# Two engines' work re-ordered around the feed-forward chunks and the norms, a weights-stationary last input stage, and an end by column halves

## The chip, the cores and the metric

The kernel runs on one core of a Trainium2 chip. The metric is the device time in microseconds (us) of one launch of the whole program; lower is better. TensorE (PE in the profile) multiplies, VectorE (DVE) and ScalarE (ACT) do the elementwise work, GpSimd (POOL) issues small loads and some elementwise work, SyncE (SP) issues the large DMAs.

## What is computed

Two transformer-like blocks on 256 tokens of width 1024, all in float32, batch 1:

```
x = x + 0.5*norm(swiglu(norm(x)))          # ffn1: 1024 -> 2*2816 -> 1024
x = x + norm(token_mixing(norm(x)))        # retention + neighbourhood attention
x = x + 0.5*norm(swiglu(norm(x)))          # ffn2
x = x + recurrent_mixer(norm(x))           # "a": 1024 -> 2*1536, conv, gated scan, -> 1024
x = x + shortconv_mixer(norm(x))           # "b"
return norm(x)

def shortconv_mixer(h):                    # WIDTH = 1536
    bg, cg, xv, gate = split(h @ w_in, 4)  # w_in is 1024 x 6144
    y = bg * causal_depthwise_conv(cg * xv, conv_w)     # 3 taps
    return (y * silu(gate)) @ w_out        # 1536 -> 1024
```

`norm` is an RMS norm over the 1024 columns with a gain.

## The kernel before

**Every product in two parts.** A float32 operand is split into a rounded high part and a low part, and a product is hi*hi + hi*lo + lo*hi, three matmuls into one accumulation. Activations sit transposed in `xT_hi` and `xT_lo` (in `xT`, side by side). All weights come as one stream of 151 groups of 1 MB (`raw`, a ring of 6 slots). ACT makes `w_hi` of a group (`round_group`, L450), then DVE makes `w_lo` in the place of `raw` (`low_group`, L872). `round_to(n)` on ACT and `low_to(n)` on DVE do all groups below n that are not done yet: where these calls stand in the two engines' programs is the order by hand that the change moves. Every engine runs its program in order and waits on semaphores (`wait_ge`). PE waits for `lo_done` before it uses a group.

**Two forms of an input stage.** In the column form (`column_tile`, matmuls L1416 to L1418) the activations of 128 tokens are stationary and 512 columns of weights stream; a column is two groups, 2 token tiles x 8 chunks x 3 = 48 matmuls of 512. The result has tokens on the partitions and has to be transposed. In the chunk form (`chunk`, L1613 and L1615) the weights are stationary: for 128 output columns, `w_hi` with `xT_hi` and `xT_lo` at once (512 wide) and `w_lo` with `xT_hi` (256 wide), 8 times; a chunk is one group, gate half and up half, 32 matmuls. Here the hi*hi+lo*hi part lies in columns 0 to 255 and the hi*lo part in 256 to 511 of the bank, and they must be added (ACT copies the second, L585 and L587; DVE adds the first, L1035 or L1038 and L1040), but nothing is transposed.

**Stages.** `f1_in` (2 columns, then 18 chunks), `f1_out`, `mix_in`, three small output stages, `f2_in`, `f2_out`, `a_in`, `a_out`, `b_in` (12 columns), `b_out`. For each chunk of `f1_in` and `f2_in`, ACT runs round_to, `chunk_round` of the chunk before (L597), `second_parts`, `chunk_silu` (L592), and DVE runs low_to, `chunk_low` of the chunk before (L1052), `chunk_sums`, `chunk_product` (L1046); in f1 the sums have one operation more (L1036, the token's scale).

**Joints.** Between stages stands `norm(n)`. PE ends the output stage with token tile t=1, transposes the normed tile t=0 within it, and starts on the next stage's first column with t=0, for which it needs `xT_hi` (ACT L460) and `xT_lo` (DVE L900, `take_lo`) of that tile. In `norm`, DVE runs `low_to(after + 3)` for t=0 ahead of the two `take_lo`. Half way through the second column's t=0 tile PE transposes the normed tile t=1 (`xn_ready`, from DVE L933).

**b_in before.** Twelve columns; ACT takes the gate (L832, L833), DVE multiplies into `b_prod` (L1357), PE transposes (`b_transposes`, L1849, 4 matmuls of 128), DVE runs the 3-tap convolution out of PSUM (L1370 to L1373), ACT and DVE make `yT_hi` and `yT_lo` (L838, L1378).

**End before.** `norm(*NORMS[5])`: for each token tile, DVE adds (L925), ACT sums squares and takes the root (L468, L470), DVE inverts (L930) and scales two halves (L933), SP stores each (L354).

## Time and profile before

| what | value |
|---|---|
| device time, median of 3 runs (lowest to highest) | 913.71 us (913.54 to 915.02) |
| the profiled execution's own time | 913.96 us |
| its span, first to last instruction | 912.2 us |
| PE busy | 897.5 us, 98% of the span, 4550 matmuls |
| PE weight loads busy | 759.2 us, 83% |
| DVE busy | 602.1 us, 66%, 742 instructions |
| ACT busy | 470.8 us, 52%, 630 instructions |
| POOL busy | 75.2 us, 8% |
| DMA | 168.87 MB, 185 GB/s on average |
| granted TensorE clock | 0.999 of full speed |

Busy time of an engine is the union of its instructions; matmuls overlap in the records, so the pace of PE is read from the starts of successive matmuls or from stretches with a known number of them. The column of a chain of waits gives for each piece what the end was waiting for.

### The profile page before, as it was taken

Reading aid. Unit: us, or ns where it says so; the run is one execution under the profiler, and the core shown is the slowest. Engines: PE = TensorE matmul, PEld = TensorE weight load, DVE = VectorE, ACT = ScalarE, POOL = GpSimd, SP = SyncE. Lnnn points to the kernel's source line nnn. Section 1 sums busy time; section 2 is a strip of 40 time slices with the busy share of each in tenths; the row PEclk is TensorE's granted clock in tenths of the full one; section 3 lists DMA queues with packets and bytes.
Section 4 is the critical chain, followed back from the end, with each engine's and each line's share of the span. In section 5 each row is a group of like instructions: output and inputs, shape, how many; then the busy total and the mean of one; then the engine's idle time right before and its main releaser. Section 6 shows DMA issues by size and latency. Waiting matters only on the chain.

```text
span 912.2 us, 11249 instructions
## 1 busy us (share of the span) xinstructions
PE 897.5 (98%) x4550; PEld 759.2 (83%) x4550; DVE 602.1 (66%) x742; ACT 470.8 (52%) x630; POOL 75.2 (8%) x103
## 2 busy tenths in 40 slices
PE   8999999999999999999999999999999999999996
PEld 6888887878888888888788888887999888888885
DVE  6677777466666646748657667446879866666653
ACT  6655556445533446435555556435787544444441
POOL 3000000003232210000000000000290000000000
PEclk9999999999999999999999999999999999999999
DMA  9755554547544534455565555546535356554421
GB/s 341 286 188 187 181 185 181 185 185 266 189 144 175 172 128 155 152 187 188 200 227 186 185 185 182 198 160 242 193 133 185 139 181 257 185 184 185 185 93 46
DMA packets 25843, 168.87 MB, mean 185 GB/s; under 512 B 3408, under 2 KB 3584, under 8 KB 6592
## 3 DMA queue, kind: packets, MB, share of 16 engines
q1 hardware_dynamic: 23040, 159.46, 47.9%
q0 software_dynamic: 2752, 8.69, 2.9%
q8 instruction: 36, 0.59, 0.3%
q14 instruction: 15, 0.12, 0.0%
HBM read 167.09 MB, written 1.05 MB: 184 GB/s over the span
## 4 chain that ended last, share of the span: by engine, by line
PE 81%; DVE 9%; ACT 6%; DMA 2%; issue 1%; SPq 0%; DVEq 0%
PE acc L1416 19%; PE acc L1418 19%; PE acc L1417 19%; PE acc L1613 7%; DVE w_lo L872 5%; ACT w_hi L450 4%; PE acc L1615 4%; PE aux L1800 1%; DMA raw<-weights 1%; PE acc L1437 1%; DVE gate_c L1036 1%; PE aux L1416 1%; PE aux L1418 1%; PE aux L1417 1%; ACT gate_c L592 1%
## 5 line engine op out<-in xcount | busy, mean ns | idle before, releaser
L872 DVE TENSOR_TENSOR w_lo<-raw,w_hi 128x2048 fp32r<-128x2048 f32 x148 | 338.5, 2302 | 161.9 <-ACT w_hi L450 161.7
L450 ACT ACTIVATE w_hi<-raw 128x2048 fp32r<-128x2048 f32 x146 | 276.4, 1911 | 51.6 <-DMA raw<-weights 51.4
L1416 PE MATMUL acc<-w_hi,xT 128*128 128x512 f32 x512 | 203.4, 397 | 2.7 <-DVE xT L900 1.7
L1613 PE MATMUL acc<-xT,w_hi 128*128 128x512 f32 x576 | 201.9, 396 | 0.0
L1418 PE MATMUL acc<-w_hi,xT 128*128 128x512 f32 x512 | 199.8, 390 | 0.0
L1417 PE MATMUL acc<-w_lo,xT 128*128 128x512 f32 x512 | 199.4, 390 | 0.0
L1615 PE MATMUL acc<-xT,w_lo 128*128 128x256 f32 x576 | 160.1, 278 | 0.0
L1613 PEld LDWEIGHTS acc<-xT,w_hi 128*128 128x128 f32 x576 | 108.0, 188 | 26.4 <-issue 1.0
L1416 PEld LDWEIGHTS acc<-w_hi,xT 128*128 128x128 f32 x512 | 96.2, 188 | 22.9 <-issue 4.1
L1418 PEld LDWEIGHTS acc<-w_hi,xT 128*128 128x128 f32 x512 | 96.1, 188 | 20.6
L1417 PEld LDWEIGHTS acc<-w_lo,xT 128*128 128x128 f32 x512 | 96.3, 188 | 18.8
L1615 PEld LDWEIGHTS acc<-xT,w_lo 128*128 128x128 f32 x576 | 108.3, 188 | 0.0
L1416 PE MATMUL acc<-w_hi,hT_hi 128*128 128x512 f32 x176 | 68.8, 391 | 1.3 <-DVE w_lo L872 1.3
L1418 PE MATMUL acc<-w_hi,hT_lo 128*128 128x512 f32 x176 | 68.5, 389 | 0.0
L1417 PE MATMUL acc<-w_lo,hT_hi 128*128 128x512 f32 x176 | 68.5, 389 | 0.0
L592 ACT ACTIVATE gate_c<-gate_c 128x256 f32<-128x256 f32 x36 | 14.9, 415 | 49.2 <-DVE gate_c L1036 46.4
L1416 PEld LDWEIGHTS acc<-w_hi,hT_hi 128*128 128x128 f32 x176 | 33.0, 188 | 8.6 <-issue 1.7
L1418 PEld LDWEIGHTS acc<-w_hi,hT_lo 128*128 128x128 f32 x176 | 33.0, 188 | 6.8
L1417 PEld LDWEIGHTS acc<-w_lo,hT_hi 128*128 128x128 f32 x176 | 33.0, 188 | 6.8
L1416 PE MATMUL acc<-w_hi,yT_hi 128*128 128x512 f32 x96 | 37.6, 392 | 0.3 <-DVE yT_lo L1293 0.3
L1815 PE MATMUL acc<-xT,w_hi 128*128 128x256 f32 x128 | 37.4, 292 | 0.0
L1418 PE MATMUL acc<-w_hi,yT_lo 128*128 128x512 f32 x96 | 37.4, 390 | 0.0
(222 smaller groups left out, 1066.4 us busy)
## 6 DMA issues: line engine op xcount, KB each, us to landing
raw<-weights SPq DMA_DIRECT2D x149, 1024.0 KB, 4.8
gain_pre<-gains POOLq DMA_DIRECT2D x5, 512.0 KB, 5.1
bias_raw<-bias_in POOLq DMA_DIRECT2D x32, 64.0 KB, 3.5
gain_post<-gains POOLq DMA_DIRECT2D x3, 512.0 KB, 4.4
gate_w<-gate_w_in POOLq DMA_DIRECT2D x1, 1536.0 KB, 8.8
x<-x_in SPq DMA_DIRECT2D x4, 256.0 KB, 5.8
raw<-weights SPq DMA_DIRECT2D x2, 512.0 KB, 5.6
out<-tmp SPq DMA_DIRECT2D x4, 256.0 KB, 2.1
```

The lines of the kernel that those rows point to most:

```text
L450: a.activation(w_hi[:, g % RING], raw[:, g % RING], ACT.Copy).then_inc(hi_done, 1)
L592: a.activation(gate_c[:, n % 2], gate_c[:, n % 2], ACT.Silu).then_inc(silu_ready, 1)
L872: v.tensor_tensor(w_lo[:, slot], raw[:, slot], w_hi[:, slot].bitcast(F32), ALU.subtract)\
L1036: v.tensor_tensor(gate_c[:, b], gate_c[:, b], rstd0_row[:], ALU.mult).then_inc(gate_summed, 1)
L1416: m.matmul(dst, hi[:, k, cols], w_hi[:, slot, w], start=first, stop=False)
L1417: m.matmul(dst, hi[:, k, cols], w_lo[:, slot, w], start=False, stop=False)
L1418: return m.matmul(dst, lo[:, k, cols], w_hi[:, slot, w], start=False, stop=last)
L1437: i = m.matmul(acc[:, t, 0], xT[:, k, t * P:(t + 1) * P], w[:, g, unit * UNIT:(unit + 1) * UNIT], start=k == 0 and xT is xT_hi and w is w_ ...
L1613: m.matmul(dst, w_hi[:, slot, w], xT[:, k].rearrange("p a q -> p (a q)"), start=k == 0, stop=False)
L1615: i = m.matmul(dst[:, 0:S], w_lo[:, slot, w], xT[:, k, 0], start=False, stop=k == KD - 1)
L1800: i = m.matmul(aux[:, 2 + ch % 2, k * S:(k + 1) * S], gate_w[:, ch, k], u[:, ch], start=True, stop=True)
L1815: m.matmul(dst, w_hi[:, slot, w], xT_hi[:, k, :], start=k == 0, stop=False)
```

## The change

It does four things. (1) In both feed-forward input stages, ACT and DVE run their work for a chunk in another order: ACT takes the gate's second part, rounds one group further ahead, then the silu, the up half's second part and the chunk's own rounding; DVE makes the gate sum, then the low part of a group, then up sum, product and the chunk's own low part. (2) In `norm`, `low_to(after + 3)` of t=0 stands behind the two `take_lo`. (3) Columns 2 to 11 of `b_in` become 20 pairs in the chunk form (`b_pair`): an even pair holds the two factors of the convolution's input, the odd one gate and `bg`; the parts are summed in `b_parts` and the convolution reads SBUF. The weights are laid out anew in HBM by the host. (4) The last token tile of the last three groups of `b_out` runs column half by column half (`last_by_halves`), and `final_norm` treats tile t=1 in halves of 512 columns, with gain times x ahead of the scale; its two stores go out from ACT's and SP's queues.

```diff
-               "f2_in": "V" * 2, "f2_out": "V", "a_in": "AA", "a_out": "V", "b_in": "V" * 12, "b_out": "V"}
+               "f2_in": "V" * 2, "f2_out": "V", "a_in": "AA", "a_out": "V", "b_in": "V" * 2, "b_out": "V"}
+B_STRAIGHT, B_PAIRS = 4, 20
...
+        elif _name == "b_in" and _g >= B_STRAIGHT:
+            RELEASE.append(("b_half", 2 * (_g - B_STRAIGHT + 1)))
...
+            for h in range(2):
+                sp.wait_ge(xn_ready, 2 * 2 * 5 + h + 1)
+                part = slice(h * DM // 2, (h + 1) * DM // 2)
+                sp.dma_start(out[0:P, part], tmp[:, 0, part]).then_inc(stored, 16)
+            sp.wait_ge(last_out_dve, 1)
+            sp.dma_start(out[P:2 * P, DM // 2:], tmp[:, 1, DM // 2:]).then_inc(stored, 16)
...
-                def second_parts(n):
+                def gate_second_part(n):
                     act.wait_ge(gate_chunk_full, c_before + n + 1)
                     if n >= 2:
                         act.wait_ge(chunk_lo, c_before + n - 1)
                     a.activation(gate_c[:, n % 2], acc[:, n % 2, 0, S:2 * S], ACT.Copy).then_inc(gate_part, 1)
+                def up_second_part(n):
                     act.wait_ge(chunk_full, c_before + n + 1)
                     a.activation(prod_c[:, n % 2], acc[:, n % 2, 1, S:2 * S], ACT.Copy).then_inc(up_part, 1)
...
+                round_to(g0 + 7)
                 for n in range(CHUNKS):
-                    round_to(g0 + 7 + n)
+                    gate_second_part(n)
+                    round_to(g0 + 8 + n)
+                    chunk_silu(n)
+                    up_second_part(n)
                     if n == 0:
                         hidden_hi(1, 1)
-                    else:
-                        chunk_round(n - 1)
-                    second_parts(n)
-                    chunk_silu(n)
-                chunk_round(CHUNKS - 1)
-                round_to(g0 + 25)
...
+            def b_second_parts(n):
+                for half in range(2):
+                    act.wait_ge(b_half_full, 2 * n + half + 1)
+                    a.activation(b_parts[:, n % 2, half], acc[:, n % 2, half, S:2 * S], ACT.Copy)\
+                        .then_inc(b_part_copied, 1)
+            def b_gate_function(n):
+                act.wait_ge(b_gate_summed, n // 2 + 1)
+                a.activation(b_parts[:, 1, 0], b_parts[:, 1, 0], ACT.Silu).then_inc(b_gate_silu, 1)
...
-            for j in range(2, 12):
-                b_column(j, j % 2, lambda: round_to(g0 + 2 * j + 4))
+            for n in range(B_PAIRS):
+                j = 2 + n // 2
+                round_to(g0 + B_STRAIGHT + 3 + n)
+                if n % 2 == 0 and n:
+                    b_hi(j - 1, (j - 1) % 2)
+                b_second_parts(n)
+                if n == 0:
+                    b_hi(1, 1)
+                if n % 2:
+                    b_gate_function(n)
...
+                act.wait_ge(x_half_ready, 1)
+                a.activation(squares[:, 0], x[:, 1, 0:DM // 2], ACT.Square, accum_out=half_sums[:, 0:1])\
+                    .then_inc(half_summed, 1)
+                act.wait_ge(x_half_ready, 2)
+                step(a.activation(squares[:, 1], x[:, 1, DM // 2:], ACT.Square, accum_out=half_sums[:, 1:2]))
+                act.wait_ge(half_bias_ready, 1)
+                a.activation(std[:, 3:4], half_sums[:, 1:2], ACT.Sqrt, bias=half_bias[:], scale=1.0 / DM)\
+                    .then_inc(pre_std, 1)
+                act.wait_ge(x_scaled_ready, 1)
+                act.wait_ge(last_rstd, 1)
+                a.activation(tmp[:, 1, 0:DM // 2], x_scaled[:, 0], ACT.Identity, bias=zero[:], scale=rstd[:, 3:4])\
+                    .then_inc(last_out_act, 1)
+                act.wait_ge(last_out_act, 1)
+                act.dma_start(out[P:2 * P, 0:DM // 2], tmp[:, 1, 0:DM // 2]).then_inc(stored, 16)
...
-                    if t == 0:
-                        low_to(after + 3)
                     if n < 5:
                         for h in range(2):
                             cols = slice(t * P, (t + 1) * P)
                             take_lo(f"t{n}", 2 * t + h, xT_lo[:, 4 * h:4 * h + 4, cols],
                                     xT_hi[:, 4 * h:4 * h + 4, cols],
                                     aux[:, 2 * t + h].rearrange("p (c q) -> p c q", c=4))
+                    if t == 0:
+                        low_to(after + 3)
...
                 for n in range(CHUNKS):
+                    chunk_gate(n)
                     low_to(g0 + 7 + n)
+                    chunk_up(n)
                     if n == 0:
                         hidden_lo(1, 1)
-                    else:
-                        chunk_low(n - 1)
-                    chunk_sums(n)
                     chunk_product(n)
-                chunk_low(CHUNKS - 1)
...
+            def b_sums(n):
+                for half in range(2):
+                    dve.wait_ge(b_part_copied, 2 * n + half + 1)
+                    part = b_parts[:, n % 2, half]
+                    i = v.tensor_tensor(part, acc[:, n % 2, half, 0:S], part, ALU.add)
+                    if half:
+                        i.then_inc(b_summed, 1)
+                    elif n % 2:
+                        i.then_inc(b_gate_summed, 1)
+                    else:
+                        step(i)
+            def b_conv_pair(n, j):
+                dve.wait_ge(b_summed, n + 1)
+                p = b_parts[:, 0, 0]
+                step(v.tensor_tensor(p, p, b_parts[:, 0, 1], ALU.mult))
+                dve.wait_ge(b_y_ready, j)
+                step(v.tensor_scalar(b_conv[:], p, tap(j, 2), None, ALU.mult))
+                step(v.scalar_tensor_tensor(b_conv[:, 1:], p[:, 0:S - 1], tap(j, 1), b_conv[:, 1:], ALU.mult, ALU.add))
+                step(v.scalar_tensor_tensor(b_conv[:, 2:], p[:, 0:S - 2], tap(j, 0), b_conv[:, 2:], ALU.mult, ALU.add))
+            def b_gated(n, j):
+                dve.wait_ge(b_summed, n + 1)
+                step(v.tensor_tensor(b_conv[:], b_conv[:], b_parts[:, 1, 1], ALU.mult))
+                dve.wait_ge(b_gate_silu, n // 2 + 1)
+                v.tensor_tensor(b_y[:, j % 2], b_conv[:], b_parts[:, 1, 0], ALU.mult).then_inc(b_y_ready, 1)
...
-            for j in range(2, 12):
-                b_column(j, j % 2, lambda: low_to(g0 + 2 * j + 4))
+            for n in range(B_PAIRS):
+                j = 2 + n // 2
+                low_to(g0 + B_STRAIGHT + 3 + n)
+                if n % 2 == 0:
+                    if n:
+                        b_lo(j - 1, (j - 1) % 2)
+                    b_sums(n)
+                    if n == 0:
+                        b_short_conv(1, 1)
+                        b_lo(1, 1)
+                    b_conv_pair(n, j)
+                else:
+                    b_sums(n)
+                    b_gated(n, j)
...
+                for h in range(2):
+                    part = slice(h * DM // 2, (h + 1) * DM // 2)
+                    if h == 0:
+                        dve.wait_ge(half_full, 1)
+                    else:
+                        dve.wait_ge(acc_full[1], b_out + 1)
+                    v.tensor_tensor(x[:, 1, part], acc[:, 1, h], x[:, 1, part], ALU.add).then_inc(x_half_ready, 1)
+                    dve.wait_ge(x_half_ready, h + 1)
+                    v.tensor_tensor(x_scaled[:, h], x[:, 1, part], gain_pre[:, part], ALU.mult)\
+                        .then_inc(x_scaled_ready, 1)
+                    if h == 0:
+                        dve.wait_ge(half_summed, 1)
+                        v.tensor_scalar(half_bias[:], half_sums[:, 0:1], 1.0 / DM, EPS, ALU.mult, ALU.add)\
+                            .then_inc(half_bias_ready, 1)
+                dve.wait_ge(pre_std, 2 * 5 + 2)
+                v.reciprocal(rstd[:, 3:4], std[:, 3:4]).then_inc(last_rstd, 1)
+                dve.wait_ge(last_rstd, 1)
+                dve.wait_ge(x_scaled_ready, 2)
+                v.tensor_scalar(tmp[:, 1, DM // 2:], x_scaled[:, 1], rstd[:, 3:4], None, ALU.mult)\
+                    .then_inc(last_out_dve, 1)
...
+            def last_by_halves(st, block, hi, lo, chunks):
+                for half in range(2):
+                    for n in block:
+                        slot = (FIRST_GROUP[st] + n) % RING
+                        for kk in range(2):
+                            k = 2 * n + kk
+                            i = product(acc[:, 1, half], hi, lo, k, 1, slot, 2 * kk + half, k == 0, k == chunks - 1)
+                    i.then_inc(acc_full[1] if half else half_full, 1)
...
-            def b_column(j, par):
-                for t in range(T):
-                    pe.wait_ge(acc_free_dve[t], n_dve - 1 + j)
-                    column_tile(g0 + 2 * j, par, t)
-                    if t == 0:
-                        b_transposes(j - 1, 1 - par)
+            def b_pair(n):
+                g = g0 + B_STRAIGHT + n
+                pe.wait_ge(lo_done, g + 1)
+                if n < 2:
+                    pe.wait_ge(acc_free_dve[n], n_dve + 2)
+                else:
+                    pe.wait_ge(b_summed, n - 1)
+                for half in range(2):
+                    dst = acc[:, n % 2, half]
+                    for k in range(KD):
+                        w = slice(2 * P * k + P * half, 2 * P * k + P * (half + 1))
+                        m.matmul(dst, w_hi[:, g % RING, w], xT[:, k].rearrange("p a q -> p (a q)"),
+                                 start=k == 0, stop=False)
+                        i = m.matmul(dst[:, 0:S], w_lo[:, g % RING, w], xT[:, k, 0], start=False, stop=k == KD - 1)
+                    i.then_inc(b_half_full, 1)
             first_columns(4, "b_in")
             b_transposes(0, 0)
-            for j in range(2, 12):
-                b_column(j, j % 2)
+            for n in range(B_PAIRS):
+                b_pair(n)
+                if n == 0:
+                    b_transposes(1, 1)
             out_stage("b_out", yT_hi, yT_lo, CH, lambda n: pe.wait_ge(bank_free, f0 + 2 * n + 2),
-                      lambda: b_transposes(11, 1))
+                      free=lambda t: pe.wait_ge(b_summed, B_PAIRS - 1 + t))
...
-    b_cols = blocks((0, 1, 3, 2), P, (0, W2))
+    b_cols = blocks((0, 1, 3, 2), P, (0, W2))[:B_STRAIGHT // 2]
+    b_pairs = np.stack([blocks(parts, P, (0, W2)) for parts in ((1, 2), (3, 0))], axis=1)[B_STRAIGHT // 2:]
+    b_pairs = b_pairs.reshape(B_PAIRS, 2 * P)
```

**ACT, the chunks of f1_in** (line numbers are those of each kernel's own program). Before, one chunk's turn and the start of the next:

```order
L450 ACTIVATE w_hi<-raw 128x2048
L597 ACTIVATE hT_hi<-prod_c 128x256
L585 ACTIVATE gate_c<-acc 128x256
L587 ACTIVATE prod_c<-acc 128x256
L592 ACTIVATE gate_c<-gate_c 128x256
L450 ACTIVATE w_hi<-raw 128x2048
```

The same place now:

```order
L608 ACTIVATE gate_c<-acc 128x256
L473 ACTIVATE w_hi<-raw 128x2048
L618 ACTIVATE gate_c<-gate_c 128x256
L613 ACTIVATE prod_c<-acc 128x256
L623 ACTIVATE hT_hi<-prod_c 128x256
L608 ACTIVATE gate_c<-acc 128x256
```

The rounding of the weights stood behind the silu of the chunk before; now it stands ahead of its own chunk's silu, and the chunk is rounded in its own turn.

**DVE, the same place.** Before, then now:

```order
L872 TENSOR_TENSOR w_lo<-raw,w_hi 128x2048
L1052 TENSOR_TENSOR hT_lo<-prod_c,hT_hi 128x256
L1035 TENSOR_TENSOR gate_c<-acc,gate_c 128x256
L1036 TENSOR_TENSOR gate_c<-gate_c,rstd_row 128x256
L1040 TENSOR_TENSOR prod_c<-acc,prod_c 128x256
L1046 TENSOR_TENSOR prod_c<-prod_c,gate_c 128x256
```

```order
L1094 TENSOR_TENSOR gate_c<-acc,gate_c 128x256
L1095 TENSOR_TENSOR gate_c<-gate_c,rstd_row 128x256
L931 TENSOR_TENSOR w_lo<-raw,w_hi 128x2048
L1103 TENSOR_TENSOR prod_c<-acc,prod_c 128x256
L1109 TENSOR_TENSOR prod_c<-prod_c,gate_c 128x256
L1115 TENSOR_TENSOR hT_lo<-prod_c,hT_hi 128x256
```

The gate sums, on which the silu waits, moved from behind the weights' low part to ahead of it.

**DVE, columns 10 and 11 of b_in**, now: an even pair, the odd pair, and the start of the next even one (before, a column had two `w_lo`, two `b_prod`, four operations of the convolution and one `yT_lo`):

```order
L931 TENSOR_TENSOR w_lo<-raw,w_hi 128x2048
L1440 TENSOR_TENSOR yT_lo<-b_y,yT_hi 128x256
L1449 TENSOR_TENSOR b_parts<-acc,b_parts 128x256 x2
L1461 TENSOR_TENSOR b_parts<-b_parts 128x256
L1463 TENSOR_SCALAR b_conv<-b_parts,conv_b 128x256
L1464 SCALAR_TENSOR_TENSOR b_conv<-b_parts,conv_b,b_conv 128x255
L1465 SCALAR_TENSOR_TENSOR b_conv<-b_parts,conv_b,b_conv 128x254
L931 TENSOR_TENSOR w_lo<-raw,w_hi 128x2048
L1449 TENSOR_TENSOR b_parts<-acc,b_parts 128x256 x2
L1470 TENSOR_TENSOR b_conv<-b_conv,b_parts 128x256
L1472 TENSOR_TENSOR b_y<-b_conv,b_parts 128x256
L931 TENSOR_TENSOR w_lo<-raw,w_hi 128x2048
```

One low part of the weights stands ahead of every pair's sums, and the convolution stands between the even pair and the odd pair's low part.

## Rows read from the trace of the kernel before

**Rows 1.** Waits of PE over the whole span: us in total, times, longest us.
```profile
PE acc L1416 <- DVE xT L900: 1.7, 2, 0.9
...
PE acc L1416 <- DVE w_lo L872: 1.3, 1, 1.3
...
PE acc L1416 <- issue: 1.0, 1, 1.0
```

**Rows 2.** Stretches of PE: from:to, length, busy (x matmuls), clock, DMA, GB/s.
```profile
72.61:135.33 62.72, 62.72 (x354) 1.00 0.53 184
457.38:463.47 6.09, 6.09 (x40) 1.00 0.66 258
463.47:469.10 5.63, 5.63 (x35) 1.00 0.53 186
469.10:557.85 88.75, 88.75 (x514) 1.00 0.54 190
758.22:871.95 113.73, 113.73 (x523) 1.00 0.50 184
871.95:882.87 10.92, 10.92 (x49) 1.00 0.40 161
```

**Rows 3.** Chain of waits, one turn of f1_in: start, us, what.
```profile
125.71 2.29 DVE w_lo L872
128.00 0.34 DVE hT_lo L1052
128.34 0.34 DVE gate_c L1035
...
128.70 0.43 DVE gate_c L1036
129.16 0.42 ACT gate_c L592
129.58 1.81 ACT w_hi L450
```

**Rows 4.** Timeline of the joint before mix_in: start, us, instruction [idle before].
```profile
196.05 1.09 ACT L460 ACTIVATE xT<-aux 128x512 fp32r<-128x512 f32 x2 [0.24 <-PE aux L1541]
...
198.05 1.28 DVE L900 TENSOR_TENSOR xT<-aux,xT 128x512 fp32r<-128x512 f32 x2
...
204.70 1.42 DVE L933 SCALAR_TENSOR_TENSOR tmp<-x,rstd,gain_pre 128x512 f32<-128x512 f32 x2
...
207.07 1.03 PE L1541 MATMUL aux<-ident_gain,tmp 128*128 128x128 f32 x8
```

**Rows 5.** Groups by form: count, busy us, mean ns, idle before.
```profile
L1371 DVE SCALAR_TENSOR_TENSOR b_conv<-aux,conv_b,b_conv 128x255 f32<-128x255 f32 x12 | 5.8, 483 | 0.4
L1378 DVE TENSOR_TENSOR yT_lo<-b_y,yT_hi 128x256 fp32r<-128x256 f32 x12 | 5.0, 416 | 1.0 <-ACT yT_hi L838 1.0
L585 ACT ACTIVATE gate_c<-acc 128x256 f32<-128x256 f32 x36 | 13.4, 371 | 0.0
L900 DVE TENSOR_TENSOR xT<-aux,xT 128x512 fp32r<-128x512 f32 x16 | 10.3, 684 | 12.1 <-ACT xT L460 12.1
```

**Rows 6.** Chain of waits at the end, behind the last matmul.
```profile
905.30 1.24 DVE x L925
...
906.56 1.16 ACT tmp L468 x2
...
907.74 0.30 ACT std L470
...
908.27 0.75 DVE tmp L933
909.02 0.66 DVEq L115
```

**Rows 7.** DMA: the four stores to landing, and the gain loads issued by POOL (KB, us).
```profile
DMA to landing us min/median/max: 2.0/2.1/2.1
...
gain_pre<-gains POOLq DMA_DIRECT2D x5, 512.0 KB, 5.1
```

More of the change, by code:

```diff
@@ L1401, in _, with final_norm @@
             low_to(FIRST_GROUP["b_out"] + 4)
[L1402 removed]
             b_lo(11, 1)
             low_to(NG)
[L1405 removed]
+            def final_norm():
+                b_out = FIRST_ACC["b_out"]
+                dve.wait_ge(gains_in, 128)
+                dve.wait_ge(acc_full[0], b_out + 1)
+                v.tensor_tensor(x[:, 0], acc[:, 0].rearrange("p h n -> p (h n)"), x[:, 0], ALU.add)\
+                    .then_inc(acc_free_dve[0], 1)
+                dve.wait_ge(pre_std, 2 * 5 + 1)
+                step(v.reciprocal(rstd[:, 2:3], std[:, 2:3]))
+                for h in range(2):
+                    part = slice(h * DM // 2, (h + 1) * DM // 2)
+                    v.scalar_tensor_tensor(tmp[:, 0, part], x[:, 0, part], rstd[:, 2:3], gain_pre[:, part],
+                                           ALU.mult, ALU.mult).then_inc(xn_ready, 1)
+                for h in range(2):
+                    part = slice(h * DM // 2, (h + 1) * DM // 2)
+                    if h == 0:
[16 more added lines that the diff above has]
+                    .then_inc(last_out_dve, 1)
@@ L1556, in out_stage @@
                             free(t)
+                        if st == "b_out" and t == 1 and block[-1] == groups - 1:
+                            last_by_halves(st, block, hi, lo, chunks)
+                            continue
                         for n in block:
```

56 lines of the change are left out of this document (31 added, 25 removed).

## Prediction

> **What bounds the kernel now.** I read the waits of PE first. In the whole span PE's idle time behind a named releaser is small: 1.3 us in front of one matmul for `w_lo`, and 1.7 us (two times) and 1.0 us (once) in front of first columns, for `xT_lo` or for "issue" [rows 1]. So PE is the bound almost everywhere, a change can gain only where PE idles, where PE does work that goes away, or behind the last matmul, and whatever else gets faster is worth nothing. Then I read PE's stretches, because a short wait at each chunk doesn't show in the waits: from chunk 7 of f1_in to the first matmul of f1_out, 11 chunks take 62.72 us, 5.70 each, while the 16 chunks of f2_in from its third on take 88.75 us, 5.55 each [rows 2]. The matmuls are the same. The chain of waits tells why: in f1 it does not run on PE at all, but round ACT and DVE: low part of the weights 2.29, chunk's low part 0.34, gate sum 0.34, scale 0.43, silu 0.42, rounding of the next weights 1.81, and some 0.08 of hand-over [rows 3]. The window I read held five such turns, and each sums to 5.71 us, the pace of the chunks. f2 lacks the scale and stays just under PE's 5.55.
>
> **Part 1, the chunks' new order.** Same instructions. The gate sum now stands ahead of the low part, and the rounding ahead of the silu, one group earlier than before. I lay the new turn out from a chunk's start: gate half full at 2.8, ACT's copy to 3.35, DVE's two sums to 4.2, low part (its rounding is done, one turn earlier) to 6.4, up sum 6.75, product 7.2, ACT's rounding of the chunk 7.7, its low part 8.1; the next gate sum is due at 5.55 + 3.35 = 8.9. What could close into a loop is DVE's own row of operations with one hand-over to ACT: about 2.2 + 0.34 + 0.43 + 0.4 + 0.4 + 0.34 + 0.43 = 4.6 us, a full 0.9 us under PE's pace. So f1 should run at f2's 5.55: 11 x 0.155 = **1.7 us**. The low part of the second group of f1_out, for which PE waits 1.3 us today, is then made in the turn of the last chunk, ready 0.9 us after f1_out starts and wanted at 2.7 us: the wait of 1.3 goes, with 0.1 to 0.2 of hand-over and slow restart: **1.4 us**. PE's demands at the start (DVE is late there by its decay rates) are met by the same laying out. In f2 nothing is gained, since PE doesn't wait. Lower bound 0 (a new loop as long as the old), upper bound 3.2.
>
> **Part 2, low parts first at joints.** DVE makes a group's low part (2.2) before the two `take_lo` (1.28 together, starting 198.05); ACT has the first high part ready at about 196.7 [rows 4]. In the new order the first `take_lo` ends near 197.4, before PE has finished its last output products, so the waits of three joints go: their idle is 1.7 + 1.0 [rows 1], with hand-over some 3.2 us. But the low part that was moved is late next: DVE is free for token tile t=1 some 0.7 us later than today, and behind that stand its norm, the next low part and the two products whose end lets PE transpose tile t=1 (204.70 + 1.42 = 206.1 today, 206.7 then). PE does those 8 transposes at 207.07 today; 1.1 us earlier it would find nothing. It gets its second half at 206.7 + 0.25, ends the transposes near 207.4 instead of 207.86, and keeps about 0.5 us [rows 4]. I take the same 0.5 for the two others, which read alike: **1.5 us**. The fourth joint (before b_in) has no wait to lose in rows 1's view; if its tile t=1 had no time to spare it would lose up to those 0.7. Bounds: 0 and 3.2.
>
> **Part 3, b_in by pairs.** Columns 2 to 11 take 113.73 us [rows 2]: 480 products and 10 blocks of 4 transposes. 48 products without transposes take 10.92 us in the same view, so a block costs (113.73 - 109.2) / 10 = 0.45 us, and 11 blocks were behind column 0's; one stays. 20 pairs are 20 chunks, and f2's stage shows their price under the same start (a block of transposes before the first and after it): 6.09 + 5.63 + 18 x 5.547 = 111.57 us [rows 2]. Gain 2.16, and 0.45 for the block of column 11, which lay in b_out: **2.6 us**. Thus almost half of what the transposes cost is eaten by the form: two matmuls of 512 and 256 take 0.347 us where one and a half of 512 take 0.341 (10.92 / 48 x 1.5), and all weight columns now come as 64 matmuls where 48 did them.
> The Trainium skill, TensorE: Matmul & The Clock Gate, section Back-to-back issue gap, gives N/2.4 + 2.5 ns per matmul; by it ten columns would take 103.6 us and twenty pairs 104.0, so the form would cost 0.4 and not 2.1 us, and the sum would come out 1.7 us lower. The trace doesn't agree (10.92 us for 48 matmuls is 227 ns each), and the rows decide.
> Cover: all other work of the stage must stay beside PE. DVE per two pairs: two low parts at 2.3, four sums, a product, two gatings and `yT_lo` at 0.42, three taps at 0.48 [rows 5]: 9.4 us of 11.09; ACT: two roundings at 1.9, four copies at 0.37, silu and `yT_hi` at 0.42: 6.1. The longest closed way round both engines I find: rounding 1.81, low part 2.3, `yT_lo` and sum 0.7, second sum and product 0.9, three taps 1.55, low part 2.2, gate sum 0.4, silu 0.4: 10.3 us. PE's 11.09 covers it by 0.8.
>
> **Part 4, the end.** The last matmul releases 4.4 us of work (add 1.24, squares 1.16, root 0.30, reciprocal with hand-over 0.23, scaled halves 0.75 and 0.66 [rows 6]), and the last store takes 2.1 and some 0.4 to the end. Now half of tile t=1 is summed 18 matmuls (4.1 us) earlier, and behind the last matmul stand: add of 512 columns 0.68 [rows 5], squares of 512 about 0.7 (half of two `xT_hi`, 0.55, and the read of the sum), root 0.30, reciprocal 0.23, and one scaling of 512 on each of two engines side by side, at most 0.75: 2.6 us. `x_scaled` of the second half (0.7) ends before the root does. Gain **1.8 us**. The store from ACT's queue is in no row: at best it lands like SP's, 2.1; at worst like POOL's gain loads, 5.1 for double the size [rows 7]. I take SP's, the same kind of queue and size, and keep 3 us for the worst. Half-major order costs PE nothing: the same 36 products.
>
> **Sum.** 1.7 + 1.4 + 1.5 + 2.6 + 1.8 = 9.0. The profiled execution took 913.96 us, 0.25 above the median of 913.71, so 904.96 by its own time and 904.7 by the median's. I forecast **904.7 us**.
>
> **Rivals.** *The b_in loop binds (slower).* If one turn round ACT and DVE is longer than 11.09 us, each 0.1 us over it costs 1.0 us in ten turns. The pairs' DVE work grew from 7.7 to 9.4 us per column, and six of its operations wait on each other. For it: the same kind of loop bound f1 unseen. Against: 10.3 by rows. It decides at 12.0 us, where the 9.0 are gone; at 12.2 the time is 915.7. Chance 0.03. A weaker form, 11.09 to 11.6, gives up to 5 us back, 905.5 to 910: 0.08. *The joints and the f1 wait move on.* The 2.9 of part 2 and of f1's wait turn up as waits further on (tile t=1, the low parts of f1_out): 906 to 908; for it, DVE's margin is 0.3 us at the first joint; against, the laying out. 0.14. *The joints keep everything,* since PE's transposes of t=1 need not wait as I think, and the end is shorter by 0.3: 904.7 - 1.7 - 0.3 = 902.7. 0.08. *The ACT store is slow:* up to 3 us at the end, 907.7: 0.06. *The order doesn't break the f1 loop* (the trace after would again show 5.7 per chunk): 907.8. 0.04. Forecast as laid out, within 1.3 us: 0.57.
>
> **How the numbers follow.** The range takes in the forecast, the first rival's near part, the joints' two sides and the slow store: 902.8 to 908.4; outside lie the binding loop and part of the bests. Measurement tells 0.2%, 1.8 us, from no change. Faster by more (under 911.9): all cases but the binding loop in its strong form: 0.95. Within 0.2%: 0.02. Slower (over 915.5): 0.03.
>
> **What would show it.** Right: f1_in at 5.55 per chunk from chunk 7 on and no turn of `w_lo`, sums, silu and `w_hi` in the chain; no wait of PE at the start of f1_out; PE's waits at the three joints gone or moved in front of the t=1 transposes with about 0.6 us each; b_in from its second block of transposes at 5.55 per pair, PE busy throughout; 2.6 us from the last matmul to the last scaled half. Wrong: pairs of b_in over 5.6 us with PE waiting for `w_lo` or `b_parts`, a chain of waits on DVE in b_in, a store that lands later than 2.1 us, or a difference spread over stages that the change doesn't touch.

## The result and the profile after

The changed kernel takes **904.41 us** in the median of four runs (904.36 to 904.64), the kernel before 913.73 (913.54 to 915.02): ratio 0.9898, 95% interval 0.9883 to 0.9912, 9.3 us faster. The forecast was 904.7, its range 902.8 to 908.4. The profiled execution after took 904.45 us with a span of 902.7, at a granted clock of 0.999.

The page's busy times, after:

```profile
PE 893.6 (99%) x4670; PEld 762.1 (84%) x4670; DVE 621.9 (69%) x785; ACT 485.7 (54%) x643; POOL 76.5 (8%) x103
```

Stretches of PE after: f1_in from chunk 7 to f1_out, 16 chunks of f2_in, all pairs of b_in, and the 48 matmuls behind them. The columns are from:to, length, busy time (x instructions) of PE, weight loads, DVE, ACT and POOL, then granted clock, DMA share and GB/s; [rows 2] shows the same view without the other engines.

```profile
72.42:133.43 61.01, 61.01 (x355) 53.35 (x353) 46.60 (x67) 36.24 (x55) 0.00 (x0) 1.00 0.54 190
464.29:553.04 88.75, 88.75 (x515) 77.62 (x514) 62.38 (x81) 52.71 (x80) 0.00 (x0) 1.00 0.54 190
752.61:864.18 111.57, 111.57 (x648) 97.55 (x647) 93.03 (x137) 57.12 (x81) 0.00 (x0) 1.00 0.55 193
864.18:875.10 10.92, 10.92 (x51) 9.02 (x50) 9.59 (x9) 9.69 (x9) 0.00 (x0) 1.00 0.27 98
```

Against [rows 2]: eleven chunks of f1_in take 61.01 us where they took 62.72, so each takes 5.55, as in f2_in, which has not moved by 0.01. The second part of b_in takes 111.57 where ten columns took 113.73. All waits of PE that the view lists after the change (us in total, times, longest us):

```profile
PE acc L1552 <- DVE warm L1041: 1.3, 1, 1.3
PE aux L1559 <- DMA x<-x_in: 0.6, 1, 0.6
PE acc L1566 <- ACT w_hi L557: 0.5, 1, 0.5
PE acc L1545 <- DVE yT_lo L1355: 0.3, 1, 0.3
PE acc L1566 <- ACT xT L547: 0.2, 1, 0.2
```

The three kinds of [rows 1] are gone. The wait for `yT_lo` stands at the start of a_out, where the kernel before has it too with 0.3 us; the other four belong to the opening, before chunk 0 of f1_in. The change touches neither place.

Since PE's matmuls are the same ones up to b_in, each can be found in both traces, and the difference of two starts in one trace and in the other says what a piece gained. These differences add up to the whole span:

| piece | before us | after us | gain | predicted |
|---|---|---|---|---|
| start to chunk 0 of f1_in | 33.16 | 32.96 | 0.20 | - |
| chunks of f1_in | 102.17 | 100.47 | 1.70 | 1.7 |
| f1_out, to its t=0 transposes | 60.08 | 58.51 | 1.57 | 1.4 |
| joint 1, to the end of t=1's transposes | 12.45 | 11.79 | 0.66 | 0.5 |
| joint 2 (with the work before it) | 106.95 | 106.27 | 0.68 | 0.5 |
| joint 3 | 12.41 | 11.60 | 0.81 | 0.5 |
| b_in's second part to the last matmul's start | 146.66 | 144.00 | 2.66 | 2.6 |
| last matmul's start to the span's end | 7.29 | 6.04 | 1.25 | 1.8 |

Gains 9.53, spans 912.17 and 902.65. The row of joint 2 starts where joint 1 ends; the joint itself, from t=0's transposes on, takes 11.60 us where it took 12.28, so the whole gain of the row lies in it. What lies between joint 3 and b_in's second part differs by 0.02 us.

The first joint in the timeline after (start, us, instruction, idle before it):

```profile
192.57 1.08 ACT L483 ACTIVATE xT<-aux 128x512 fp32r<-128x512 f32 x2 [0.66 <-PE aux L1680]
193.20 1.29 DVE L959 TENSOR_TENSOR xT<-aux,xT 128x512 fp32r<-128x512 f32 x2 [2.80 <-ACT xT L483]
194.41 2.28 DVE L931 TENSOR_TENSOR w_lo<-raw,w_hi 128x2048 fp32r<-128x2048 f32 x1
...
201.84 1.42 DVE L992 SCALAR_TENSOR_TENSOR tmp<-x,rstd,gain_pre 128x512 f32<-128x512 f32 x2
...
202.65 1.32 PE L1680 MATMUL aux<-ident_gain,tmp 128*128 128x128 f32 x8
```

DVE's `take_lo` starts 0.63 us after ACT's high part; in [rows 4] it started 2.00 us after it, behind a low part of weights. That low part now comes next, and PE's transposes of t=1 start 0.8 us after DVE's norm of t=1, where 2.4 us lay between the two starts in [rows 4].

The end after, behind the last matmul (start 896.61):

```profile
897.04 0.69 DVE L1519 TENSOR_TENSOR x<-acc,x 128x512 f32<-128x512 f32 x1 [2.10 <-PE acc L1547]
897.77 0.63 ACT L908 ACTIVATE squares<-x 128x512 f32<-128x512 f32 x1 [3.01 <-DVE x L1519]
...
898.52 0.29 ACT L910 ACTIVATE std<-half_sums,half_bias 128x1 f32<-128x1 f32 x1
898.85 0.16 DVE L1528 RECIPROCAL rstd<-std 128x1 f32<-128x1 f32 x1 [0.39 <-ACT std L910]
899.05 0.49 DVE L1531 TENSOR_SCALAR tmp<-x_scaled,rstd 128x512 f32<-128x512 f32 x1
899.11 0.81 ACT L914 ACTIVATE tmp<-x_scaled,zero,rstd 128x512 f32<-128x512 f32 x1 [0.29 <-DVE rstd L1528]
...
899.95 0.37 ACTq L917 DMA_DIRECT2D out<-tmp  x1
```

From the add's start to the last scaled half it is 2.88 us, and the later half is ACT's, whose scaling takes 0.81 where DVE's takes 0.49.

### The profile page after: what moved, and what is told of

Its sections match the earlier page's. It is cut to its first block, busy times and chain, and to the rows that moved or that the text cites. A ratio compares the mean times of both kernels' runs of the same rounds, so it can differ in the third digit from the quotient of the medians.

```text
span 902.7 us, 11537 instructions
## 1 busy us (share of the span) xinstructions
PE 893.6 (99%) x4670; PEld 762.1 (84%) x4670; DVE 621.9 (69%) x785; ACT 485.7 (54%) x643; POOL 76.5 (8%) x103
## 4 chain that ended last, share of the span: by engine, by line
PE 94%; DVE 3%; ACT 2%; issue 1%; DMA 1%; SPq 0%; DVEq 0%; ACTq 0%
PE acc L1545 16%; PE acc L1547 16%; PE acc L1546 16%; PE acc L1755 15%; PE acc L2007 8%; PE acc L1757 7%; PE acc L2009 4%; PE aux L1942 1%; PE acc L1566 1%; PE aux L1680 1%; PE aux L1545 1%; PE aux L1547 1%; PE aux L1546 1%; PE aux L1797 1%; PE aux L1847 1%; PE acc L1957 1%
## 5 line engine op out<-in xcount | busy, mean ns | idle before, releaser
L1755 PE MATMUL acc<-xT,w_hi 128*128 128x512 f32 x576 | 200.4, 394 | 0.0
L1757 PE MATMUL acc<-xT,w_lo 128*128 128x256 f32 x576 | 159.7, 277 | 0.0
L1545 PE MATMUL acc<-w_hi,xT 128*128 128x512 f32 x352 | 139.9, 398 | 0.0
L1547 PE MATMUL acc<-w_hi,xT 128*128 128x512 f32 x352 | 137.4, 390 | 0.0
L1546 PE MATMUL acc<-w_lo,xT 128*128 128x512 f32 x352 | 137.1, 390 | 0.0
L1755 PEld LDWEIGHTS acc<-xT,w_hi 128*128 128x128 f32 x576 | 108.0, 188 | 24.9
L2007 PE MATMUL acc<-xT,w_hi 128*128 128x512 f32 x320 | 111.3, 394 | 0.0
L1757 PEld LDWEIGHTS acc<-xT,w_lo 128*128 128x128 f32 x576 | 108.2, 188 | 0.0
L2009 PE MATMUL acc<-xT,w_lo 128*128 128x256 f32 x320 | 88.7, 277 | 0.0
L1547 PEld LDWEIGHTS acc<-w_hi,xT 128*128 128x128 f32 x352 | 66.1, 188 | 14.2
L1545 PEld LDWEIGHTS acc<-w_hi,xT 128*128 128x128 f32 x352 | 66.2, 188 | 13.5 <-issue 0.6
L1546 PEld LDWEIGHTS acc<-w_lo,xT 128*128 128x128 f32 x352 | 66.2, 188 | 12.9
L2007 PEld LDWEIGHTS acc<-xT,w_hi 128*128 128x128 f32 x320 | 60.0, 188 | 13.9
L2009 PEld LDWEIGHTS acc<-xT,w_lo 128*128 128x128 f32 x320 | 60.1, 188 | 0.0
```

The lines of the kernel that those rows point to most:

```text
L1545: m.matmul(dst, hi[:, k, cols], w_hi[:, slot, w], start=first, stop=False)
L1546: m.matmul(dst, hi[:, k, cols], w_lo[:, slot, w], start=False, stop=False)
L1547: return m.matmul(dst, lo[:, k, cols], w_hi[:, slot, w], start=False, stop=last)
L1755: m.matmul(dst, w_hi[:, slot, w], xT[:, k].rearrange("p a q -> p (a q)"), start=k == 0, stop=False)
L1757: i = m.matmul(dst[:, 0:S], w_lo[:, slot, w], xT[:, k, 0], start=False, stop=k == KD - 1)
L2007: m.matmul(dst, w_hi[:, g % RING, w], xT[:, k].rearrange("p a q -> p (a q)"), start=k == 0, stop=False)
```

## The experiments

In the diffs `-` is the changed kernel and `+` the experiment, but for the one that starts from the kernel before; `...` stands for lines left out. Stretches are taken from the profiled execution of each. A median of four can stand off its profiled execution by 1 to 2 us here; the section on the hardware comes back to that.

### Each part undone by itself

**Chunk order, u1.**

```diff
                 for n in range(CHUNKS):
-                    chunk_gate(n)
                     low_to(g0 + 7 + n)
-                    chunk_up(n)
...
+                    chunk_sums(n)
                     chunk_product(n)
```

(and ACT's loop as before)

> The changed kernel (904.4 us) with the order of ScalarE and VectorE inside a feed-forward chunk put back as it was before, all else as changed. Theory (the parts add up as in the ledger of TensorE's stretches): feed-forward 1 goes back from 5.55 to 5.70 us per chunk from about chunk 7 on, 1.7 us, and TensorE's wait of 1.3 to 1.5 us at the first output chunk returns with some 0.2 more behind it: 3.3 us longer, about 907.7 us. Rival (the joint behind feed-forward 1 takes up the loss, since a later TensorE finds its operands ready): 1.5 to 2 us longer, 906 to 906.4. A second rival (the order inside the chunks does nothing, the other parts made the whole gain): no change.

Measured: 907.96 us (907.62 to 908.34). Its stretch and the wait:

```profile
72.93:135.69 62.76, 62.76 (x354) 53.71 (x353) 45.56 (x66) 33.68 (x56) 0.00 (x0) 1.00 0.53 184
```

```profile
PE acc L1540 <- DVE w_lo L929: 1.3, 1, 1.3
```

The chunks of f1_in take 102.21 us (1.74 more) and f1_out 60.11 (1.60 more): 3.34, and f2_in, the joints, b_in and the end agree with the changed kernel within 0.03. The opening took another 0.52 in this execution. The f1_out part holds PE's wait for `w_lo` again. The joints take up nothing; both rivals fall.

**Joints, u2.**

```diff
+                    if t == 0:
+                        low_to(after + 3)
                     if n < 5:
...
-                    if t == 0:
-                        low_to(after + 3)
```

> The changed kernel (904.4 us) with the low parts of column 4 of the next stage put back ahead of the low parts that its first product needs, at the three joints, all else as changed. Theory: TensorE's three waits at the joints return with about 1.1, 0.65 and 0.35 to 0.8 us, 2.1 us in sum, about 906.5 us. The prediction's own size for this part was 0.5 at each joint: 1.5, 905.9 us. Rival (the gain at the joints came from the chunks' order, which leaves VectorE earlier there): no change.

Measured: 906.57 us (905.83 to 908.25). The waits are back:

```profile
PE acc L1545 <- DVE xT L959: 1.9, 2, 1.0
...
PE acc L1545 <- issue: 0.6, 1, 0.6
```

The three joints cost 0.34, 0.81 and 0.87 us more, 2.0 in sum. The first is cheaper than the 0.66 of the table. There the wait depends on the chunks too: from t=0's transposes to the first matmul behind them PE took 3.42 us before, 3.02 here, and 3.07 in c3 below, which also has the old joint and no chunk loop. So if the low part stays in its old place, the chunk order alone gives some 0.35 us of the first joint's gain. The rival is thus right for half of one joint and wrong for the rest.

**Columns, u3** (b_in's ACT, DVE and PE loops, banks and weight layout as before).

```diff
-            for n in range(B_PAIRS):
-                b_pair(n)
-                if n == 0:
-                    b_transposes(1, 1)
+            for j in range(2, 12):
+                b_column(j, j % 2)
```

> The changed kernel (904.4 us) with the last input stage put back to whole columns, all else as changed. Theory: 16 first pairs at 5.68 us for each column instead of pairs at 5.55 us, 2.2 us, and the 0.45 us of the end that the ledger gives to this part: 2.65 longer, about 907.1 us. Rival (the stage's pace of before was VectorE's and a part of the gain came from the other parts, which let it start earlier): under 1.5 us longer.

Measured: 907.89 us (907.17 to 909.21), profiled 907.38. The stage's start lies 719.67 us behind chunk 0 of f1_in as in the changed kernel (719.65), its second part takes 113.73 us again, and from there to the last matmul 0.50 more: 2.66, as expected. The columns' pace is the same 113.73 us although the kernel ahead of them is now the changed one, and PE is busy throughout; so the gain is the form's and not an earlier start's. The median lies 3.5 us above the changed kernel's: its executions spread from 907.17 to 909.21, and the profiled one is near the low end.

**End, u4** (`last_by_halves` and `final_norm` undone, stores from SP).

```diff
-                    v.tensor_tensor(x[:, 1, part], acc[:, 1, h], x[:, 1, part], ALU.add).then_inc(x_half_ready, 1)
...
-                a.activation(tmp[:, 1, 0:DM // 2], x_scaled[:, 0], ACT.Identity, bias=zero[:], scale=rstd[:, 3:4])\
```

> The changed kernel (904.4 us) with the last output stage and the last norm put back to whole width in place of column halves, all else as changed. Theory: the stretch from the last product's start to the end goes from 6.1 back to 7.3 us, 1.25 us longer, about 905.65 us. The prediction's size was 1.8: 906.2 us. Rival (halves and whole width differ by less, because the two column halves cost TensorE more): 0.5 us longer or less.

Measured: 906.02 us (905.88 to 907.83). The last matmul starts 144.00 us behind b_in's first pair in both, so halves cost PE nothing, and the end takes 7.30 where it took 6.04: 1.26.

The four by themselves are 3.34 + 2.02 + 2.66 + 1.26 = 9.28 us of the 9.33 that lie behind the opening. By profiled stretches the parts are additive within 0.1 us; the first joint's 0.3 us less is made up by about 0.1 each at the two other joints and in the chunks. By medians the four cost 3.5, 2.2, 3.5 and 1.6 us, 10.8 in sum for a gain of 9.3: the executions that lie 1 to 2 us high, of which the last section tells, are in them.

### What the chunk order does

**DVE's order alone, c1.** ACT's program is the old one.

```diff
-                    gate_second_part(n)
-                    round_to(g0 + 8 + n)
-                    chunk_silu(n)
-                    up_second_part(n)
+                    round_to(g0 + 7 + n)
...
+                    second_parts(n)
+                    chunk_silu(n)
```

> The changed kernel (904.4 us) with ScalarE's order inside a chunk put back as before, VectorE's as changed. Theory (the wait ran in a loop through both engines, and one cut is enough): chunks stay at 5.55 us, 904.4 us, no change within 0.4 us. Rival (both engines must be reordered for the loop to be shorter than TensorE's 5.55 us): 5.6 to 5.70 us per chunk and up to 3.3 us longer, 906 to 907.7 us.

**ACT's order alone, c2.** DVE makes the sums behind the low part again.

```diff
                 for n in range(CHUNKS):
-                    chunk_gate(n)
                     low_to(g0 + 7 + n)
-                    chunk_up(n)
+                    if n:
+                        chunk_low(n - 1)
+                    chunk_sums(n)
```

> The changed kernel (904.4 us) with VectorE's order inside a chunk put back as before, ScalarE's as changed; one low part of chunk 1 is moved behind chunk 0's sums so that the order can run. Theory (one cut is enough): 904.4 us, no change within 0.4 us. Rival (both needed, or VectorE's order is the one that counts): 5.6 to 5.70 us per chunk, 906 to 907.7 us.

Measured: 904.45 us (904.23 to 906.41) and 904.38 (904.35 to 906.28). The stretch from chunk 7 on, of c1, then of c2:

```profile
72.48:133.49 61.01, 61.01 (x355) 53.36 (x353) 45.93 (x67) 34.74 (x55) 0.00 (x0) 1.00 0.54 190
```

```profile
72.37:133.38 61.01, 61.01 (x354) 53.36 (x353) 46.65 (x69) 36.77 (x57) 0.00 (x0) 1.00 0.54 190
```

The same time to 0.01 us. This turn, which passes through two engines, is cut by reordering either one; half of part 1 is redundant.

**The loop made shorter in the kernel before, c3.**

```diff
-                        step(v.tensor_tensor(gate_c[:, b], acc[:, b, 0, 0:S], gate_c[:, b], ALU.add))
-                        v.tensor_tensor(gate_c[:, b], gate_c[:, b], rstd0_row[:], ALU.mult).then_inc(gate_summed, 1)
+                        v.tensor_tensor(gate_c[:, b], acc[:, b, 0, 0:S], gate_c[:, b], ALU.add).then_inc(gate_summed, 1)
```

> The kernel before (913.7 us) without ScalarE's scaling of the gate by the token's scale in the chunks of feed-forward 1, an operation of 0.44 us per chunk; this part of the computation is left out. Theory (the 5.70 us per chunk are a loop of ScalarE and VectorE that closes above TensorE's 5.55): the loop is 5.70 less 0.44 = 5.26 and TensorE sets 5.55 us per chunk; the wait at the first output chunk goes as well: 3.2 us shorter, about 910.5 us. Rival (5.70 is TensorE's or its operands' own pace): no change, 913.7 us.

(The operation is VectorE's, L1036; the expectation names the wrong engine. This kernel leaves out the token's scale on the gate, and nothing else.) Measured: 910.46 us (910.18 to 910.92) beside 913.63, so 3.17 less.

```profile
72.94:133.96 61.02, 61.02 (x355) 53.35 (x354) 43.22 (x58) 34.86 (x55) 0.00 (x0) 1.00 0.54 190
```

One operation of 0.43 us per chunk out of the turn, and PE's own pace is back without any new order. That the turn of [rows 3] set the 5.70 us is shown, both by cutting it and by shortening it.

### Where the margin of b_in ends

**Two and four more operations, d2 and d4** (d4 has `range(4)`).

```diff
+                for _ in range(2):
+                    step(v.scalar_tensor_tensor(squares[:, 0, 0:S], p, tap(j, 0), b_conv[:], ALU.mult, ALU.add))
```

> The changed kernel (904.4 us) with two more VectorE operations of 256 columns in each second pair of the last input stage, about 1.0 us more per two pairs; their results are not used. Theory (the loop of ScalarE and VectorE is about 10.5 us per two pairs against TensorE's 11.09, so 11.5 is over it by 0.4, and TensorE's operands stand 4 us or more ahead, which ten turns do not use up): 0 to 0.5 us longer. Rival (no such reserve: each turn's excess is paid): 4 to 4.6 us longer, 908.4 to 909 us. The prediction's rival that this loop already binds: 10 us longer.

> The same with four more VectorE operations, about 2.0 us per two pairs. Theory: the loop is about 12.5 us against TensorE's 11.09, 1.4 us over in each of ten turns, less the 4.4 us by which the operands stand ahead: 10 us longer, about 914 us. Rival (each turn pays in full): 14 to 15 us longer. Rival (VectorE alone counts, busy well below TensorE's time): no change.

Measured: 909.85 us (908.18 to 910.14; profiled 908.18) and 922.67 (920.11 to 923.55; profiled 923.01). The forecasts of 0 to 0.5 and of 10 us are both wrong, and no rival's number fits either: d2 is 3.7 us longer by its profiled execution and 5.4 by its median, d4 18 to 19. (d2's three other executions, 909.75 to 910.14, were not profiled.) DVE's low part of an even pair, once per turn of two pairs, in the timelines of the changed kernel, of d2 and of d4:

```profile
765.22 2.29 DVE L931 TENSOR_TENSOR w_lo<-raw,w_hi 128x2048 fp32r<-128x2048 f32 x1
...
806.26 2.29 DVE L931 TENSOR_TENSOR w_lo<-raw,w_hi 128x2048 fp32r<-128x2048 f32 x1
...
817.29 2.29 DVE L931 TENSOR_TENSOR w_lo<-raw,w_hi 128x2048 fp32r<-128x2048 f32 x1
```

```profile
766.17 2.29 DVE L931 TENSOR_TENSOR w_lo<-raw,w_hi 128x2048 fp32r<-128x2048 f32 x1
...
867.89 2.29 DVE L931 TENSOR_TENSOR w_lo<-raw,w_hi 128x2048 fp32r<-128x2048 f32 x1
```

```profile
769.07 2.29 DVE L931 TENSOR_TENSOR w_lo<-raw,w_hi 128x2048 fp32r<-128x2048 f32 x1
...
867.79 2.29 DVE L931 TENSOR_TENSOR w_lo<-raw,w_hi 128x2048 fp32r<-128x2048 f32 x1
```

In the changed kernel four turns lie between the first two rows: 10.26 us each, the turn's own length, since DVE there makes up its lateness from the stage's start and its only waits are for ACT's `w_hi`; then 11.03 to the third row and 11.09 for each turn behind it, PE's pace. In d2 nine turns take 101.72, 11.30 each, in d4 eight take 98.72, 12.34 each. Two operations lengthen the turn by 1.04, twice: 10.26, 11.30, 12.34. So the loop is real, and 0.83 us under PE's time. What was wrong is the reserve. In the changed kernel the low part of b_out's second group is ready at 863.95 and wanted at 866.92, 3.0 us ahead, a margin that DVE's shorter turn earns inside the stage. In d2 that low part starts 6.3 us later, counted from the stage's start, and PE itself comes only 1.35 later, so 2.0 us of wait are left, and PE meets them in b_out:

```profile
870.33 0.47 PE L1547 MATMUL acc<-w_hi,yT_hi 128*128 128x512 f32 x1 [1.98 <-DVE w_lo L931]
```

d2's 3.62 us, counted from b_in's first pair to the last matmul, are this wait with its restart, 2.27, and 1.35 within b_in, for which see the last section. In d4, 16.8 us:

```profile
PE acc L2009 <- DVE b_parts L1449: 7.2, 9, 1.0
PE acc L1547 <- DVE w_lo L931: 3.0, 1, 3.0
```

```profile
879.00:883.00 4.00, 0.99 (x4) 0.59 (x3) 3.89 (x6) 0.20 (x1) 0.00 (x0) 0.84 0.48 199
883.00:889.00 6.00, 6.00 (x16) 4.65 (x16) 4.90 (x5) 6.00 (x6) 0.00 (x0) 0.54 0.00 0
889.00:892.00 3.00, 3.00 (x15) 2.49 (x14) 3.00 (x3) 2.98 (x2) 0.00 (x0) 1.00 0.03 5
```

b_in costs 10.7 more (nine waits of 0.8 for the sums that free the bank, and a slower pace between), then 3.0 of wait in b_out, and behind it 2.9 us because the granted clock stands at about half (the level of 1.2 GHz): twelve matmuls of 512 in a row start 0.427 us apart instead of 0.227, with a slow one at either end. The remaining 1.8 us of d4's profiled execution lie in f1_in, which the edit doesn't touch (see the last section).

### What was left at the joints and at the end

**Both last stores from SP, e1.**

```diff
+            sp.wait_ge(last_out_act, 1)
+            sp.dma_start(out[P:2 * P, 0:DM // 2], tmp[:, 1, 0:DM // 2]).then_inc(stored, 16)
...
-                act.wait_ge(last_out_act, 1)
-                act.dma_start(out[P:2 * P, 0:DM // 2], tmp[:, 1, 0:DM // 2]).then_inc(stored, 16)
```

> The changed kernel (904.4 us) with both stores of the last output tile issued by SyncE instead of one by ScalarE. Theory (the store from ScalarE's queue landed 2.3 us after its issue, those from SyncE's 2.1, and the last one ends the program): 0.2 us shorter, 904.2 us. Rival (the second store waits behind the first in SyncE's queue): 0 to 0.3 us longer.

Measured: 904.59 us (904.32 to 905.08), the same. Stores in the changed kernel (KB, median us to landing):

```profile
out<-tmp SPq DMA_DIRECT2D x3, 256.0 KB, 2.1
...
out<-tmp ACTq DMA_DIRECT2D x1, 256.0 KB, 2.3
```

From the issue of the last store to the span's end it is 2.70 us in both kernels. The queue makes no difference, and a median over other stores did not price the last one. What goes with the longer landing is how closely the store follows the one ahead of it. In the kernel before, in c3 and in u4 the last store is issued 0.66 to 0.67 us behind its neighbour and lands in 2.06 to 2.07 us; in the changed kernel and in all other experiments it is issued 0.39 us behind and lands in 2.30, from either queue (in d2 2.52, where its neighbour took 0.23 more as well). No run changes this spacing alone, so that it is the cause is not shown.

**Transposes of t=1 later, e2.** Six matmuls more of the second column stand ahead of them, at three joints.

```diff
+                        if late and half == 1 and unit == 2:
+                            late()
...
-                column_tile(g0 + 2, 1, 0, lambda half: run(1) if half else None)
+                if n == 4:
+                    column_tile(g0 + 2, 1, 0, lambda half: run(1) if half else None)
+                else:
+                    column_tile(g0 + 2, 1, 0, late=lambda: run(1))
```

> The changed kernel (904.4 us) with the transposes of the norm of the second token tile issued six products (1.36 us) later at each of the three joints. Theory (TensorE still stands 0.3 to 0.5 us at each joint, waiting for the normed tile at these transposes; later, they find it ready): 1.1 us shorter, 903.3 us. Rival (what TensorE waits for moves on to the operands of the next stage, which become ready that much later): no change or up to 1 us longer.

**Both diffs together, e3.**

> The two edits together. Theory: 1.3 us shorter, 903.1 us, the fastest of all. Rival: only the store's 0.2 us, 904.2 us.

Measured: 903.48 us (903.24 to 904.05) and 903.59 (903.49 to 903.66). In e2, between the starts of stretches away from the moved matmuls, joint 1 gives 0.57 us, joint 2 0.27 and joint 3 0.29: 1.14, where 1.1 was expected. DVE's norm of t=1 and the transposes now:

```profile
202.10 1.41 DVE L992 SCALAR_TENSOR_TENSOR tmp<-x,rstd,gain_pre 128x512 f32<-128x512 f32 x2
```

```profile
203.97 1.03 PE L1682 MATMUL aux<-ident_gain,tmp 128*128 128x128 f32 x8
```

They take 1.03 us as before the change instead of 1.32, with no idle time ahead. The second half is ready at 203.51, 0.46 before they begin. e3 adds nothing to e2, since the store gave nothing. e2 is the fastest kernel here: 10.2 us under the kernel before (ratio 0.9890, 0.9875 to 0.9904) and 0.9 under the changed one by medians.

## Why the prediction was right

It was right in its time and, in the main, in its steps.

- **What bounds.** Right. Every gain in the table but the opening's 0.20 is PE's idle time, PE's own work or the end, and c1 and c2 move work on ACT or DVE at no change.
- **Part 1.** Right, mechanism and size: 1.70 for 1.7 and 1.57 for 1.4. The turn read in [rows 3] as 5.71 us lost 0.43 in c3 and PE's pace came back. The laying out from a chunk's start didn't see that one engine's order would do.
- **Part 2.** The mechanism is right, the size was off: 2.15 for 1.5. "PE ends the transposes near 207.4 instead of 207.86" gave 0.5 for each joint; they gave 0.66, 0.68 and 0.81. That a new wait stands at t=1's transposes is shown by e2, which removed it for 1.1 us. The 0.5 was also taken over for joints 2 and 3 because they "read alike"; they don't quite, and e2 gained half as much there as at joint 1.
- **Part 3.** Right: 2.16 in the stage, as predicted, and 0.50 for column 11's block where 0.45 was put. u3 alone gives it back whole. The rule of the Trainium skill, TensorE: Matmul & The Clock Gate, section Back-to-back issue gap, would have made the pairs' gain 1.7 larger; the section gives its formula for a single matmul apart from the weight loads, and the trace after does not agree with it here: 111.57 us for twenty pairs, the price of f2's rows.
- **Part 4.** The failed term: 1.25 for 1.8. Halves cost PE nothing, as said (u4). But "one scaling of 512 on each of two engines side by side, at most 0.75" took 0.81 on ACT, and the chain from the add to the last half 2.88 instead of 2.6. (The prediction's own terms add to 2.66. Of the 0.22 beyond them this scaling is 0.06, and the rest lies in the hand-overs between the two engines and in the squares.) The other 0.24 us lie behind the last scaled half: from it to the span's end it was 2.49 us and is 2.73, a stretch that the sum took to be the same. It is 2.73 with the store from SP too (e1), so the queue isn't the cause. It goes with the closer issue of the last two stores (see e1); whether that is the cause stays open. The store that ACT issues landed in 2.3 us, so the rival of a slow one, up to 3 us, did not come.
- **The rivals.** The b_in loop was read as 10.3 us and is 10.26 by the first turns after the change and by d2 and d4; it covers by 0.83. "Each 0.1 us over it costs 1.0 us in ten turns" and "It decides at 12.0 us" are too kind: at 11.30 the kernel loses 3.6 us up to its last matmul, at 12.34 16.8, where the rule gives 2.1 and 12.5. Inside b_in the loss is even under the rule (1.35 and 10.7); what comes on top is the next stage's wait, and in d4 the lower clock behind it.
- **The opening** gave 0.20, which no step had; over all kernels here chunk 0 starts between 32.88 and 33.49 us with nothing ahead of it changed, so it is scatter.

The errors (joints +0.65, f1_out +0.17, b_in +0.06, the opening +0.2, the end -0.55) partly cancel. By the profiled executions the sum came out 9.5 for 9.0, by the medians 9.3; that the forecast was met to 0.3 us is in part luck.

## What to carry to other kernels

When a stage's pace is a little above another's with the same matmuls, first compare the distances between the starts of successive matmuls, since they alone can differ (last section). If they don't explain it, follow the chain of waits once round: if one turn over several engines sums to the pace, it is the suspect. Here one operation taken out of it, or a new order on either of its two engines, was enough, and the gain ended where PE's own pace began. A margin per turn is also what pays for the lateness at the next stage's start, so price a longer turn there as well. When a piece of work is moved ahead on an in-order engine, look for what is now late and move its consumer too: here six matmuls of delay at each of three joints gave 1.1 us.

## What the hardware showed that I had not expected

**The same matmuls run at two paces.** In u2's profiled execution f1_in took 102.28 us in place of 100.47 with no part of that stage changed and no wait in it:

```profile
73.03:135.21 62.18, 62.18 (x355) 53.93 (x353) 46.60 (x67) 36.21 (x55) 0.00 (x0) 1.00 0.53 186
```

That is 5.65 us per chunk, not 5.55, at a granted clock of 1.00. The starts of successive matmuls of 512 and 256 columns lie 231, 112, 233, 117 ns apart in the one case, over and over (346.5 per two), and 240, 120, 236, 114, 232, 118 in the other (353.3 per two). Four and six starts, of the changed kernel and of u2:

```profile
59.94 0.39 PE L1755 MATMUL acc<-xT,w_hi 128*128 128x512 f32 x1
60.17 0.27 PE L1757 MATMUL acc<-xT,w_lo 128*128 128x256 f32 x1
60.28 0.40 PE L1755 MATMUL acc<-xT,w_hi 128*128 128x512 f32 x1
60.51 0.28 PE L1757 MATMUL acc<-xT,w_lo 128*128 128x256 f32 x1
```

```profile
59.95 0.40 PE L1755 MATMUL acc<-xT,w_hi 128*128 128x512 f32 x1
60.19 0.28 PE L1757 MATMUL acc<-xT,w_lo 128*128 128x256 f32 x1
60.31 0.40 PE L1755 MATMUL acc<-xT,w_hi 128*128 128x512 f32 x1
60.55 0.28 PE L1757 MATMUL acc<-xT,w_lo 128*128 128x256 f32 x1
60.66 0.40 PE L1755 MATMUL acc<-xT,w_hi 128*128 128x512 f32 x1
60.89 0.28 PE L1757 MATMUL acc<-xT,w_lo 128*128 128x256 f32 x1
```

In all stages read here a pattern holds until PE is interrupted, and what comes then can be either. Every f1_in and f2_in has the slow one in chunk 0; behind the four transposes the fast one follows in most profiles, and the slow one for the rest of f1_in in u2's and d4's. In d2 a gap of 0.2 us at 803.2 was followed by the slow one for the rest of b_in, and most of its 1.35 us there are this. So there a wait of 0.2 us was followed by a loss of about 1.15, six times itself. In the kernel before, f1_in's later chunks show both patterns, and nearly every chunk from chunk 8 on takes 5.69 to 5.72 us with either: the loop filled the rest. Single executions some 2 us above their neighbours (908.25 in u2, 909.21 in u3, 906.41 in c1, 906.28 in c2, 907.83 in u4, and three of d2's four) are of the size of one stage at the slow pattern, 1.8 us in f1_in; of these only u2's was profiled, so for the rest it is not shown, nor is it shown what chooses the pattern.

**The clock after a wait.** With d4's wait of 3.0 us the granted clock fell to about half and stayed there for 6 us. Behind d2's wait of 1.98 us, in the same place, it stayed at 1.00:

```profile
870.33:880.00 9.67, 9.67 (x43) 7.99 (x44) 8.56 (x9) 9.42 (x8) 0.00 (x0) 1.00 0.01 2
```

So did the clock between the 0.8 us waits of d4. The longer wait thus cost 2.9 us on top of itself. The two kernels also differ in those nine waits ahead of it, so it is not shown that the length of the last one alone decides.

**ACT's scaling** of 512 columns by a value per partition took 0.81 us against DVE's 0.49 for the same shape, side by side, from the two halves of one tile.
